# Low parts of every second late expert input tile on GpSimd, counted with VectorE's

## What is computed

```python
s1, i1 = lax.top_k(s[:, :, 0], PEER_TOPK)
s2, i2 = lax.top_k(s[:, :, 1], PEER_TOPK)
cand = (s1[..., :, None] + s2[..., None, :]).reshape(T, PEER_HEADS, PEER_TOPK * PEER_TOPK)
cand_idx = (i1[..., :, None] * N_KEYS + i2[..., None, :]).reshape(T, PEER_HEADS, PEER_TOPK * PEER_TOPK)
top_s, pos = lax.top_k(cand, PEER_TOPK)
idx = jnp.take_along_axis(cand_idx, pos, axis=-1)
w = jax.nn.softmax(top_s, axis=-1)
...
act = jax.nn.gelu(jnp.einsum('cd,chkd->chk', x_c, u[idx_c]).astype(jnp.float32), approximate=False)
coef = (w_c * act).astype(v.dtype)
return jnp.einsum('chk,chkd->cd', coef, v[idx_c])
```

## Time and profile before

| what | value |
|---|---|
| median of 3 runs | 1875.97 us (1873.82 to 1881.62) |
| the profiled execution | 1873.37 us |
| its span, first to last instruction | 1871.4 us |
| busy share of PE, PEld, DVE, ACT, POOL | 90%, 80%, 65%, 47%, 4% |
| mean granted clock of TensorE over the span | 0.933 of 2.4 GHz |
| bytes moved, mean rate | 230.04 MB, 123 GB/s |

### The profile page before, as it was taken

One profiled execution on the slowest core, in us unless ns is written; L12 is line 12 of the kernel. 1 busy time (PEld: TensorE's weight loads), 2 busy tenths in 40 slices (PEclk: granted clock), 3 DMA queues, 4 the chain that ended last, 5 costly groups with the idle time before them and its releaser, 6 DMA issues. The chain is left out here.

```text
span 1871.4 us, 34461 instructions
## 1 busy us (share of the span) xinstructions
PE 1680.2 (90%) x13190; PEld 1488.5 (80%) x13190; DVE 1212.1 (65%) x2127; ACT 885.5 (47%) x1539; POOL 71.0 (4%) x35
## 2 busy tenths in 40 slices
PE   5989987899999999989999999596986999899968
PEld 5978786899999999988888888494454989788856
DVE  4556565489988899986666666544534656655554
ACT  3335543254545666656666666342432644233323
POOL 0000000100000000000000000000000333100000
PEclk9979998999999999999999999696577999999989
DMA  5532153455555333336666666350012444200004
GB/s 173 177 113 83 54 158 112 137 173 164 180 170 178 123 114 114 113 124 192 192 193 195 192 191 193 105 170 23 1 45 68 136 152 153 91 3 3 3 24 135
DMA packets 62790, 230.04 MB, mean 123 GB/s; under 512 B 6976, under 2 KB 7232, under 8 KB 62544
## 3 DMA queue, kind: packets, MB, share of 16 engines
q1 hardware_dynamic: 62672, 228.39, 38.9%
HBM read 227.32 MB, written 1.05 MB: 122 GB/s over the span
## 5 line engine op out<-in xcount | busy, mean ns | idle before, releaser
L987 DVE TENSOR_TENSOR tile_low<-weights,tile_high 128x1024 fp32r<-128x1024 f32 x252 | 307.1, 1221 | 146.6 <-ACT tile_high L977 142.9
L977 ACT ACTIVATE tile_high<-weights 128x1024 fp32r<-128x1024 f32 x252 | 268.2, 1064 | 136.4 <-issue 136.4
L172 ACT ACTIVATE tile_high<-weights 128x1024 fp32r<-128x1024 f32 x169 | 177.8, 1057 | 275.3 <-PE banks L219 120.2
L184 DVE TENSOR_TENSOR tile_low<-weights,tile_high 128x1024 fp32r<-128x1024 f32 x146 | 177.7, 1224 | 192.7 <-ACT tile_high L172 165.4
L219 PE MATMUL banks<-parts,tile_high 128*128 128x272 f32 (+1 forms) x1904 | 269.2, 296 | 27.1 <-PEq L264 18.0
L219 PEld LDWEIGHTS banks<-parts,tile_high 128*128 128x128 f32 x1904 | 251.4, 197 | 43.9 <-issue 35.9
L1039 PE MATMUL banks<-parts,tile_high 128*128 128x256 f32 x2048 | 272.0, 286 | 7.1 <-PEq L913 7.1
L1039 PEld LDWEIGHTS banks<-parts,tile_high 128*128 128x128 f32 x2048 | 256.4, 193 | 7.3 <-issue 7.3
L1324 PE MATMUL banks<-tile_high,parts 128*128 128x512 f32 x1024 | 254.7, 391 | 4.6 <-ACT parts L1304 4.6
L1324 PEld LDWEIGHTS banks<-tile_high,parts 128*128 128x128 f32 x1024 | 193.2, 189 | 45.0 <-issue 4.8
L1044 PE MATMUL banks<-parts,tile_low 128*128 128x256 f32 x1024 | 148.6, 288 | 21.5 <-DVE tile_low L987 21.5
(11 more groups left out here) (341 smaller groups left out, 2001.5 us busy)
## 6 DMA issues: line engine op xcount, KB each, us to landing
weights<-in_peer_u SPq DMA_DIRECT2D x128, 512.0 KB, 3.5
weights<-in_peer_v SPq DMA_DIRECT2D x128, 512.0 KB, 3.5
weights<-in_dn_in SPq DMA_DIRECT2D x49, 512.0 KB, 3.5
weights<-in_in_t SPq DMA_DIRECT2D x19, 512.0 KB, 3.6
weights<-in_attn_t SPq DMA_DIRECT2D x19, 512.0 KB, 3.5
weights<-in_in_m SPq DMA_DIRECT2D x16, 512.0 KB, 3.7
weights<-in_wq SPq DMA_DIRECT2D x16, 512.0 KB, 3.6
weights<-in_dn_out SPq DMA_DIRECT2D x16, 512.0 KB, 3.6
```

Source lines behind the costliest of these rows:

```text
L172: k.nc.scalar.activation(k.high[:, m % 2, :], k.ring.view(n), ACT.Copy).then_inc(*k.high_made.up())
L184: unit.tensor_tensor(k.low[:, m % 2, :], k.ring.view(n), k.high[:, m % 2, :].bitcast(F32), ALU.subtract).then_inc(*k.low_made[engine].up())
L977: k.nc.scalar.activation(k.high[:, (s + j) % 2, :], k.ring.buf[:, j % RING, :], ACT.Copy).then_inc(k.high_made.sem, 1)
L987: k.nc.vector.tensor_tensor(k.low[:, (s + j) % 2, :], k.ring.buf[:, j % RING, :], k.high[:, (s + j) % 2, :].bitcast(F32), ALU.subtract).th ...
```

## The change

A range `aside` holds every second tile from 84 to 126, 22 tiles. VectorE skips their low parts, and GpSimd makes them at L1270, with the waits that VectorE's had, and a further one: the count of low parts must show that tile n-1's is made. Since both engines now raise one count, VectorE's low parts from tile 83 on get the same further wait. Other consumers of the count are unchanged. All waits stand for the order of the count: low part n is started when low part n-1 is complete, whichever engine made that.

```diff
--- before.py
+++ after.py
@@ -1017,6 +1017,7 @@
     wide = lambda ap: ap.unsqueeze(2).broadcast_to([P, NT * PH, TOPK])
     iota = k.c("iota")
     picked = []
+    aside = range(opened + 1, NKEY - 1, 2)
     with nc.Block() as block:
 
         @block.sync
@@ -1168,6 +1169,8 @@
                 picked.append(pick.total)
 
             def low(n):
+                if n >= opened:
+                    dve.wait_ge(low_made.sem, low0 + n)
                 fori_low(dve, k, first, n // BODY, n % BODY)
 
             def choose():
@@ -1242,7 +1245,7 @@
             for g in beside(opened):
                 make(g)
             for n in range(opened, NKEY + 1):
-                if n < NKEY:
+                if n < NKEY and n not in aside:
                     low(n)
                 for g in beside(n + 1):
                     make(g)
@@ -1260,6 +1263,12 @@
             for tt in range(NT):
                 pool.wait_ge(pick.sem, picked[tt])
                 nc.gpsimd.memset(blocks(LOOPED // BODY + 4 + tt, 1), 1.0).then_inc(*ones.up())
+            for n in aside:
+                pool.wait_ge(k.high_made.sem, s + n + 1)
+                pool.wait_ge(used.sem, first + n - 1)
+                pool.wait_ge(low_made.sem, low0 + n)
+                nc.gpsimd.tensor_tensor(k.low[:, (s + n) % 2, :], ring.buf[:, n % RING, :],
+                                        k.high[:, (s + n) % 2, :].bitcast(F32), ALU.subtract).then_inc(low_made.sem, 1)
     after_fori(k)
     used.total += NKEY
     gelu.total += NKEY
```

## The result

The changed kernel took 1897.60 us (median of 6 runs, 1897.2 to 1898.87), the kernel before 1876.78 (median of 6, 1873.08 to 1881.62). The ratio is 1.0112, with a 95% interval of 1.0096 to 1.0129: slower by about 21 us. The profiled execution took 1897.49 us with a span of 1895.6; against the profiled one of before that is 24.1 us more.

What follows compares the result with a forecast made beforehand. VectorE was taken to bound the late low parts; 22 holds of 2.32 to 2.39 us less 1.13 saved give about +27 us, so 1873.37 becomes 1900.4 and, with the runs' median 2.6 higher, 1902; range 1862 to 1912, the forecast's own 1895 to 1912.

Steps and rivals of the forecast that it cites:

- The bound: Late low parts, tiles 83 to 127: VectorE sets the pace, 9.39 us per two tiles against TensorE's 8.32.
- Removed: 22 low parts leave VectorE in the late stretch, 1.13 us each, 24.9 us in all.
- The decision, who gets in between two one-hots: After VectorE's low part: GpSimd enters after the first one-hot and the second waits, 2.39 us less up to 0.07.
- The rival in which GpSimd stands back: GpSimd starts only after the run of one-hots, with the merge: -10 us, 1864 to 1866; chance 0.15.
- no collision: One-hots go free beside GpSimd's subtraction and TensorE sets the pace: -18 us, 1855 to 1858; chance 0.12.
- What collides: VectorE instructions all in SBUF (one-hots, low parts) exclude GpSimd's subtraction, whole instructions at a time; those with a PSUM input are untouched.
- second case: Earlier row at 1554.00: VectorE TENSOR_TENSOR of 16x272 beside GpSimd's subtraction took 0.85 us, its like right after 0.43.
- the first case: Earlier row at 1490.70: VectorE TENSOR_SCALAR of only 128x40 beside GpSimd's subtraction lasted 2.16 us.
- the price of one hold: Each GpSimd low part holds a VectorE one-hot in the late stretch for 2.32 to 2.39 us.
- the +27: Sum over the late stretch: 22 x (2.32 to 2.39 - 1.13) = 26.2 to 27.7 us slower.
- What was said to cost nothing: VectorE's further wait, later ScalarE high parts and SyncE loads, TensorE's waits (about 2.3 us per two tiles), later one-hots.
- The clock: Rival: longer waits drop TensorE to 1.2 GHz; only if it stays low, 16.6 us a pair, +160 in all; chance 0.03.

Runs made afterwards that it cites:

- the late start under cover: The change, with GpSimd's low parts also waiting for the step's last one-hot and VectorE's merge and folds ahead of its one-hots at those tiles: 1858.70 us, ratio 0.9902.

## Why the prediction was right

**The bound.** VectorE set the pace, and with 22 low parts fewer and nothing held it would have been TensorE: the late start under cover has the predicted 181 us (180.3), with TensorE busy throughout.

**Removed.** 1.13 us for a low part, as predicted. From the start of a low part to the start of VectorE's next instruction the traces have 49.8 us for the 44 low parts before, and 24.9 for the 22 that the change left. The one-hots, counted in the same way, went from 74.7 to 122.3 us. 47.6 more and 24.9 less are 22.7 of the 23.1 us.

**GpSimd's duration and start.** 2.39 us of work, and a start 0.16 us after VectorE's low part against the 0.1 of the prediction: both nearly as said, and inside the first one-hot.

**The decision, who gets in between two one-hots.** GpSimd did, after the first, in 21 of 22 steps with a duration of 2.65 to 2.69 us. Only for tile 84 did it ask during the second of two one-hots, so that a merge covered part of it, and the four one-hots behind the merge took 4.15 us, 1.66 more. The Trainium skill, GPSIMD Engine Reference, Key points, names contention with Vector instructions that have two SBUF inputs; the runs agree, with 2.19 us for a one-hot and nothing for merges and folds. The note in the Trainium skill, Advanced Engine Details and Errata, Mode Summary, speaks of two-port instructions only and would by itself have let the one-hots go free, and the measurement decides against that reading. The rival in which GpSimd stands back was wrong for the change. Made to start late, GpSimd gained as that rival had it, but 5.5 us and not 10. The other rival, no collision, was wrong too.

**What collides** was drawn too wide. The prediction counted every VectorE instruction that reads and writes only SBUF. The trace of the kernel before has one that went free, right ahead of its second case, with GpSimd's low part from 1552.16 to 1554.56:

```profile
1552.13 1.83 DVE L1421 RECIPROCAL rows<-rows 16x272 f32<-16x272 f32 x1
```

It took 1.83 us beside GpSimd, which took its usual 2.40; a reciprocal of 20x272 at 1280.7 us, with GpSimd idle, took 1.84. It has one input. The one-hots, the low parts and the instruction of the second case have two inputs in SBUF, and each kind collided where it met GpSimd's subtraction. Of those with one input in SBUF, the reciprocal did not collide and the TENSOR_SCALAR of the first case did; what parts those two is not shown. For this change it made no difference, since the one-hots have two.

**The term that was mis-sized** is the price of one hold, "2.32 to 2.39", which was 2.18 to 2.19. 22 times 0.17 is 3.7 of the 3.9 us by which the +27 was too large against the stretch's +23.1. The prediction took off 0.07 for the gap between one-hots, by a pace of 1.07 us for 1024 columns that no row shows. The rest, 0.13 us, can be seen at the end of a hold: the held one-hot ended 0.55 us after GpSimd's low part (638.78 and 638.23), though one lasts 0.68 alone. So its work would have begun 0.13 us before the recorded end of GpSimd's; that is worked out and not tested. Against the medians, 1902 was 4.4 us too high: 1876.78 + 23.1 would be 1899.9, and the other 2.3 us are less than the scatter of the runs of before.

**What was said to cost nothing** cost nothing: in the waits of the stretch no engine waits for a loaded tile, only GpSimd waits for a high part, once at its start, and VectorE never waits for GpSimd's count. TensorE's waits for a low part grew to 1.2 us on average (23.7 by 19) and 2.7 at most, where 2.3 had been forecast for each pair of tiles.

**The clock.** This rival came true in part and cost nothing. Two windows of the changed kernel:

```profile
640.00:660.00 20.00, 17.57 (x147) 17.16 (x147) 19.42 (x24) 10.87 (x29) 5.34 (x2) 1.00 0.38 108
680.00:700.00 20.00, 15.71 (x119) 15.15 (x118) 19.29 (x23) 13.23 (x33) 5.34 (x2) 0.93 0.31 103
```

The granted clock is 1.00 at 640 us and 0.93 at 680, 0.96 over the stretch where it was 1.00. In the timeline of TensorE in the second:

```profile
689.80 1.12 PE L1045 MATMUL banks<-parts,tile_low 128*128 128x256 f32 x8
...
691.57 2.15 PE L1040 MATMUL banks<-parts,tile_high 128*128 128x256 f32 x16
696.40 1.51 PE L1045 MATMUL banks<-parts,tile_low 128*128 128x256 f32 x8 [2.68 <-DVE tile_low L987]
```

After a wait of 2.68 us the eight matmuls took 1.51 us, where those at 689.80 took 1.12: for a part of them TensorE was at the lower level, 1.2 GHz. VectorE's 19.42 and 19.29 of 20 us hardly change with it, and its own sum above accounts for 22.7 of the 23.1 us: what TensorE lost lay in its own waits.

## What to carry to other kernels

Before work goes from VectorE to GpSimd, sort VectorE's instructions there into those that GpSimd's will hold and those that it won't, and see which will run at the moment when GpSimd starts. Here those with two inputs in SBUF were held and those with one input in PSUM were not; of two with a single input in SBUF one was held and one was not. Beside the first kind, GpSimd's instruction cost VectorE nearly its own length, which was twice what it saved; beside the second kind it was free. So choose the moment, by one more wait and by the order of VectorE's program: the same 22 subtractions made this kernel 1.1% slower or 1.0% faster.

## What the runs showed that was not expected

A copy on GpSimd with one input held one-hots as the subtraction did, 0.84 us for each. A memset on GpSimd, which reads nothing, held no low part. In the changed kernel:

```profile
484.59 1.21 DVE L987 TENSOR_TENSOR tile_low<-weights,tile_high 128x1024 fp32r<-128x1024 f32 x1
484.73 1.81 POOL L1265 MEMSET big<- 128x2048 f32 x1 [110.04 <-DVE kept L1167]
```

Both took their usual time, the memset 1.81 us as before. This is one place, and no run was made for it.

The trace counts a held VectorE instruction as busy, so the collision shows nowhere as a wait: not in the waits, and in the busy share only as more work. It has to be read from the longest of equal instructions: the 128 one-hots have a median of 684 ns and a maximum of 2887.

TensorE's clock fell five times in the stretch, though TensorE was busy 199.19 of 224 us: during or right after the low-part matmuls that followed waits of 2.68 us (at 696.40), 2.69 (757.38 and 828.85), 1.86 (778.39) and 1.80. The last of these:

```profile
717.35 1.88 PE L1045 MATMUL banks<-parts,tile_low 128*128 128x256 f32 x8 [1.80 <-DVE tile_low L987]
```

After a wait of 1.82 us at 645.94 it did not fall. In the window of 20 us around that place, shown above, the granted clock is 1.00. So the length of the last wait alone does not decide it here.
